# Two pairs of projection chunks by seven products instead of eight, the value section last

## What is computed

```python
z = _rmsnorm(x, norm_g) @ w_in                       # (512 + 8, 1024) @ (1024, 4096)
rq, rk, rv, rg, sq, sk, sv, sg = jnp.split(z, 8, axis=-1)
rq = _rope(rq.reshape(b, l, H_RET, HEAD_DIM), pos)   # rk likewise
o_ret, s_new = _retention(rq, rk, rv, s0)
sq = _rmsnorm(sq.reshape(b, l, H_SB, HEAD_DIM), sb_qn_g)   # sk likewise
o_sb = _sb_attention(sq, k_all, v_all, pos, k_pos)   # samples: paged key and value cache, 64 pages each
mix = jnp.concatenate([o_ret * jax.nn.silu(rg), o_sb * jax.nn.silu(sg)], axis=-1)
return x + mix @ w_out, s_new, sk, sv
```

## Time and profile before

| what | value |
|---|---|
| median of three runs | 962.53 us |
| the profiled execution, its own time | 960.3 us |
| its span, first to last instruction | 958.7 us |
| PE, DVE, ACT, POOL busy | 911.0, 480.1, 293.2, 249.2 us |
| the projection of layer 0, first matmul to last row | 10.1 to 253.2 us |
| mean granted TensorE clock | 0.985 |

### The profile page before, as it was taken

The page is one execution under the profiler, slowest core; times in us unless marked ns, Lnnn a source line. Parts: engine busy times, 40 slices in busy tenths (PEclk is TensorE's granted clock), DMA queues, the critical chain, the costliest instruction groups (busy, mean ns, idle before and its releaser), DMA issues.

```text
span 958.7 us, 15899 instructions
## 1 busy us (share of the span) xinstructions
PE 911.0 (95%) x5224; PEld 484.8 (51%) x5224; DVE 480.1 (50%) x965; ACT 293.2 (31%) x716; POOL 249.2 (26%) x353
## 2 busy tenths in 40 slices
PE   8999999999899999999999999998899998887998
PEld 4444444444455553545565676566554444444444
DVE  1248777779344643212133262724677775776211
ACT  6111111103454541032101110433565564655000
POOL 0000223200033430340424242000443354357000
PEclk9999999999999999999999999999899997999999
DMA  9333666593154457782414142030122232033211
GB/s 356 105 126 119 226 226 192 189 287 79 45 147 158 138 193 271 255 195 91 135 42 146 34 143 87 13 90 12 42 60 66 65 94 97 1 92 108 92 45 45
DMA packets 82487, 117.61 MB, mean 123 GB/s; under 512 B 21006, under 2 KB 45790, under 8 KB 82094
## 3 DMA queue, kind: packets, MB, share of 16 engines
q1 hardware_dynamic: 61824, 78.87, 25.2%
q0 software_dynamic: 10944, 29.41, 10.4%
q10 hardware_dynamic: 9648, 8.41, 2.7%
HBM read 108.70 MB, written 11.36 MB: 125 GB/s over the span
## 4 chain that ended last, share of the span: by engine, by line
PE 84%; DVE 6%; DMA 3%; ACT 3%; issue 2%; POOL 1%; POOLq 1%; SPq 0%; ACTq 0%; DVEq 0%
PE ps L729 26%; PE ps L989 11%; PE ps L995 6%; PE ps L1293 6%; PE ps L1012 4%; PE ps L738 4%; PE ps L1051 3%; PE ps L927 3%; PE ps L1163 3%; PE ps L1174 3%; DMA arena<-cache_sb_v 2%; PE ps L905 2%; DVE work L2000 2%; PE ps L877 2%; PE ps L1029 1%
## 5 line engine op out<-in xcount | busy, mean ns | idle before, releaser
L729 PE MATMUL ps<-wring,arena 128*128 128x512 f32 x448 | 195.3, 594 | 1.5 <-issue 1.5
L729 PEld LDWEIGHTS ps<-wring,arena 128*128 128x128 f32 x448 | 84.1, 190 | 104.0 <-issue 103.9
L668 POOL TENSOR_TENSOR z<-z,work 128x1024 f32<-128x1024 f32 (+1 forms) x64 | 80.1, 1254 | 159.6 <-DVE work L2008 159.3
L989 PE MATMUL ps<-wring,z 128*128 128x512 f32 (+2 forms) x320 | 106.7, 488 | 0.0
L1525 ACT ACTIVATE z<-ps,work 128x512 f32<-128x512 f32 (+3 forms) x128 | 66.4, 525 | 72.0 <-DVE work L2000 69.8
L1348 ACT ACTIVATE z<-ps 128x512 f32<-128x512 f32 (+1 forms) x64 | 27.4, 433 | 181.8 <-PE ps L729 147.5
L360 POOL DMA_DIRECT2D arena<-cache_sb_k x64 | 34.4, 537 | 164.1 <-DVE work L1643 141.6
L989 PEld LDWEIGHTS ps<-wring,z 128*128 128x128 f32 x320 | 54.8, 190 | 43.4 <-issue 41.8
L1848 DVE TENSOR_TENSOR arena<-ps,consts 128x512 f32<-128x512 f32 x32 | 30.3, 1020 | 82.3 <-PE ps L1029 82.3
L1805 DVE TENSOR_TENSOR xres<-xres,ps 128x512 f32<-128x512 f32 (+1 forms) x32 | 15.5, 484 | 86.4 <-PE ps L1293 38.9
L1012 PE MATMUL ps<-arena,wring 64*128 64x512 f32 (+3 forms) x256 | 54.3, 502 | 4.2 <-ACT z L1525 4.2
(11 more groups left out here) (322 smaller groups left out, 1272.5 us busy)
## 6 DMA issues: line engine op xcount, KB each, us to landing
wring<-w_in SPq DMA_DIRECT2D x12, 2048.0 KB, 11.1
arena<-cache_sb_k POOLq DMA_DIRECT2D x64, 256.0 KB, 3.1
arena<-cache_sb_v SPq DMA_DIRECT2D x64, 256.0 KB, 3.7
wring<-w_out SPq DMA_DIRECT2D x3, 2048.0 KB, 7.9
arena<-cache_sel_k SPq DMA_DIRECT2D x64, 64.0 KB, 1.8
consts<-aux SPq DMA_DIRECT2D x1, 2315.5 KB, 15.1
xres<-x_prompt SPq DMA_DIRECT2D x4, 512.0 KB, 8.0
wring<-w_in SPq DMA_DIRECT2D x2, 1024.0 KB, 7.1
```

What stands on the lines that cost most here:

```text
L668: nc.gpsimd.tensor_tensor(P_u(n), P_u(n), bc(coef(n).unsqueeze(2), [P, 2, (NT - n % NT) * P]), ALU.mult).then_inc(n_scaled, 1)
L729: mm = pe.matmul(ps[:, t, 0:width], stat, mov, start=(k == 0), stop=(k == KT - 1))
L989: mm = pe.matmul(ps[:, bank, at:at + w], normed1(k, t), wring[:, slot, k, lo:lo + w], start=(k == 0), stop=(k == KT - 1))
```

## The change

The sections are renumbered: SQ, SK, SG, RQ, RK, RV, RG and SV last. The pairs (SQ, SK) and (RQ, RK) are computed by Strassen's scheme in Winograd's form: x is cut into two token halves and two k halves (A11, A12, A21, A22), the two sections' weights into quarters of 1 MB (b11, b21, b12, b22), and seven products of 256 tokens x 512 k x 512 columns stand for eight. A product is two token tiles of four matmuls. VectorE makes four sums of x once (S1 to S4), four sums of weights per pair (T1, T2, T3, T4) and ten sums of 512 columns of products per pair. The other sections are computed as before. Other edits:

- The key pages are issued by SP, and two pages share one product and one reduction on VectorE; the page loop is cut into five parts with the second pair's sums between them.
- SP's order: after the second pair's weights (mm_done waits) the first key pages, half of RV's weights, all other key pages, the retention state, the first value pages, the samples' retention values; then o4 and o6; o5 and o7 after SV is evicted; then o3 and the other value pages.
- ACT's queue issues the other quarters of RV, RG and SV. SG's and half of RV's weights lie in parts of z that are not yet written.
- SV is computed last, in banks 5 and 4 by turns, with `sb_turn(0, 0)` before it, `front(0)` after its tile 0, `front(1)` after tile 1, `rs_turn` and `ds_sums` after tile 2. The copies of q and k go to ACT; `softplus(0)` goes to DVE's place after `rotate(RK)`; the sample's softplus chain stands between the two rotations. In the loop's first step `rs_sums` stands behind the retention's first turn.

```diff
-SQ, SK, SV, SG, RQ, RK, RV, RG = range(8)
+SQ, SK, SG, RQ, RK, RV, RG, SV = range(8)
...
 # SP
+                sp.wait_ge(mm_done, MM_PAIR[0] + 14)
+                for q, section, half in ((3, RK, 1), (2, RK, 0)):
+                    quarter_load(q, section, half)
+                sp.wait_ge(mm_done, MM_PAIR[0] + 16)
+                for half in range(2):
+                    quarter_load(half, RQ, half)
+                load_pages(sp, "cache_sb_k", page_loaded, 0, 0, 1)
+                sp.wait_ge(mm_done, MM_PLAIN[SG] + 5)
...
+                load_pages(sp, "cache_sb_k", page_loaded, 0, 1, NB * NPG // 4)
                 sp.wait_ge(ds_scores, 1)
...
+                sp.wait_ge(sections_ready, 2)
+                store(outs["o4"]..., z[:, 0:NT, SK * HW:(SK + 1) * HW])
+                store(outs["o6"]..., sec(NT, SK))
+                sp.wait_ge(bank_free, 5 + 5 * NCHUNK0)
+                store(outs["o5"]..., z[:, 0:NT, SV * HW:(SV + 1) * HW])
+                store(outs["o7"]..., sec(NT, SV))
                 sp.wait_ge(rs_S, 1)
...
 # PE
+                def product(bank, x, w, t, onto=False):
+                    for k in range(KT // 2):
+                        mm = pe.matmul(ps[:, bank, :], xpart(x, k, t), w[:, k], start=(k == 0 and not onto), stop=(k == KT // 2 - 1),
+                                       skip_group_check=True)
+                    mm.then_inc(mm_done, 1)
+                def pair(p):
+                    free, loads = FREE_PAIR[p], 16 * (p + 1)
+                    made, before = DVE_PAIR[p], DVE_PAIR[0]
+                    pe.wait_ge(q_loaded[0], loads)
+                    for t in range(2):
+                        if p == 0:
+                            turn_x(0, t)
+                            pe.wait_ge(xnT_ready, t + 1)
+                        else:
+                            pe.wait_ge(bank_free, FREE_PLAIN[SG] + t + 1)
+                        product(t, "A11", quarter(0), t)
+                    pe.wait_ge(q_loaded[1], loads)
+                    for t in range(2):
+                        if p == 0:
+                            turn_x(0, 2 + t)
+                        pe.wait_ge(bank_free, free + 1 + t)
+                        product(t, "A12", quarter(1), t, onto=True)
+                    if p == 0:
+                        turn_x(0, NT)
+                        pe.wait_ge(xnT_ready, NT + 1)
...
+                    plain_rows(4, from_quarters(0, 1))
...
+                    plain_rows(5, from_quarters(2, 3))
+                    pe.wait_ge(dve_sum, 1 if p == 0 else before + 8)
+                    for t in range(2):
+                        product(2 + t, "S4", quarter(3), t)
+                    pe.wait_ge(dve_sum, made + 1)
+                    for t in range(2):
+                        pe.wait_ge(dve_sum, before + 9 + t) if p else None
+                        product(6 + t, "S3", t3_sum, t)
+                    pe.wait_ge(dve_sum, made + 2)
+                    for t in range(2):
+                        pe.wait_ge(bank_free, free + 7 + t)
+                        product(2 + t, "S1", quarter(2), t, onto=True)
+                    pe.wait_ge(dve_sum, made + 3)
+                    for t in range(2):
+                        pe.wait_ge(bank_free, free + (6, 5)[t])
+                        product((5, 4)[t], "S2", quarter(0), t)
+                    pe.wait_ge(dve_sum, made + 4)
+                    for t in range(2):
+                        pe.wait_ge(bank_free, free + 9 + t)
+                        product(6 + t, "A22", quarter(1), t, onto=True)
...
+                pair(0)
+                plain(SG, from_sections, freed_by_pair(0), turned_out=True)
+                pair(1)
+                plain(RV, from_section_and(3), freed_by_pair(1))
+                plain(RG, from_quarters(2, 0), lambda t: (bank_free, FREE_PLAIN[RV] + t + 1))
+                sb_turn(0, 0)
                 for t in range(NT):
+                    pe.wait_ge(bank_free, FREE_PLAIN[SV] + (0, 0, 1, 2)[t])
+                    plain_tile(SV, t, 5 - t % 2, w_sv)
+                    if t == 0:
+                        front(0)
                     if t == 1:
+                        front(1)
+                    if t == 2:
                         rs_turn()
                         ds_sums()
+                plain_rows(5, w_sv)
                 pe.wait_ge(zeroed, 1)
                 pe.wait_ge(ds_a, 1)
...
 # DVE
+                st.done(TT(xsum["S1"], half[2], half[3], ALU.add))
+                st.done(TT(xsum["S2"], xsum["S1"], half[0], ALU.subtract))
+                turned_x(0, NT)
+                st.done(TT(xsum["S4"], half[1], xsum["S2"], ALU.subtract))
+                TT(xsum["S3"], half[0], half[2], ALU.subtract).then_inc(dve_sum, 1)
+                weight_sums(0, 0, 4)
...
+                pair_sums(0, 0)
+                pair_sums(0, 1)
                 head_norm(SQ, "gain_sq")
+                def page_products(first, last):
+                    with st.loop(last - first, 2, first=first) as r:
+                        for v in range(2):
+                            for u in (2 * v, 2 * v + 1):
+                                dve.wait_ge(page_loaded[u], r * 16 + 16)
+                            TT(work[:, 0:2 * CH]..., pages[:, 2 * v:2 * v + 2, :], bc(qbc..., [P, 2, CH]), ALU.mult).then_inc(page_free, 2)
+                            dve.wait_ge(page_free, r * 4 + (4 + 2 * v + 2))
+                            st.done(RED(zs[:, ...], heads(work[:, 0:2 * CH]), AX.X, ALU.add))
                 head_norm(SK, "gain_sk")
+                weight_sums(1, 0, 1)
+                page_products(0, 3)
+                weight_sums(1, 1, 4)
+                page_products(3, 7)
+                pair_sums(1, 0)
+                page_products(7, 8)
+                pair_sums(1, 1)
+                page_products(8, NB * NPG // 4)
                 TS(zs, zs, SCALE, None, ALU.mult).then_inc(ds_scores, 1)
                 rotate(RQ, 3)
...
+                rotate(RK, 4)
+                softplus(0)
```

```diff
+                leave(sec(0, SV), ps[:, 5, :], m + 1)
                 tail_of(0)
+                leave(sec(1, SV), ps[:, 4, :], m + 2)
+                leave(sec(2, SV), ps[:, 5, :], m + 3)
+                act.wait_ge(ds_la, 1)
+                tail_of(1)
+                leave(sec(3, SV), ps[:, 4, :], m + 4)
+                leave_rows(SV, 5, m + 5)
                 act.wait_ge(ds_lasum, 1)
                 nc.scalar.activation(zs, zs, ACT.Exp).then_inc(ds_a, 1)
-                tail_of(1)
```

More of the change, by code:

```diff
@@ L748, in project, with plain_tile @@
                     project_rows(n, slot, turned, before, width)
-                def second_half():
-                    pe.wait_ge(w_loaded[0], 16)
-                    turn_x(0, 1)
+                def plain_tile(section, t, bank, weights, turned_out=False):
+                    for k in range(KT):
+                        if turned_out:
+                            stat, mov = weights(k)[:, t * P:(t + 1) * P], xnT[:, k, 0:SEQ]
+                        else:
+                            stat, mov = by_token(k, t), weights(k)
+                        mm = pe.matmul(ps[:, bank, :], stat, mov, start=(k == 0), stop=(k == KT - 1))
+                    mm.then_inc(mm_done, 1)
@@ new lines, in plain_rows @@
+                def plain_rows(bank, weights):
+                    for k in range(KT):
+                        for row, a, e in quarters(0, CH):
+                            mm = pe.matmul(ps[row:row + NB, bank, 0:e - a], xnT[:, k, SEQ:SEQ + NB], weights(k)[:, a:e],
+                                           start=(k == 0), stop=(k == KT - 1))
+                    mm.then_inc(mm_done, 1)
+                def product(bank, x, w, t, onto=False):
+                    for k in range(KT // 2):
+                        mm = pe.matmul(ps[:, bank, :], xpart(x, k, t), w[:, k], start=(k == 0 and not onto), stop=(k == KT // 2 - 1),
+                                       skip_group_check=True)
+                    mm.then_inc(mm_done, 1)
@@ new lines, in leave, with leave_rows @@
+                def leave(dst, src, event, func=ACT.Copy):
+                    act.wait_ge(mm_done, event)
+                    nc.scalar.activation(dst, src, func).then_inc(bank_free, 1)
+                def leave_rows(section, bank, event):
+                    act.wait_ge(mm_done, event)
+                    for row, a, e in quarters(0, CH):
+                        ins_ = nc.scalar.activation(sec(NT, section)[:, a:e], ps[row:row + NB, bank, 0:e - a],
+                                                    ACT.Silu if section in (SG, RG) else ACT.Copy)
+                    ins_.then_inc(bank_free, 1)
@@ new lines, in pair @@
+                def pair(p):
+                    (sA, sB), m = PAIRS[p], MM_PAIR[p]
+                    if p:
+                        for t in range(2):
+                            leave(sec(2 + t, sB), ps[:, t, :], m + 1 + t)
+                    for t in range(2):
```

(19 more changed lines are left out.)

301 lines of the change are left out of this document (189 added, 112 removed).

## The result

The changed kernel takes **968.41 us** (median; 963.63 to 973.8) against 961.83 for the kernel before on the same chip: a ratio of 1.0068 [1.0048, 1.0089]. 968 was predicted, in a range of 957 to 977; the sign (slower) holds too, though by little over the half per cent that can be told. The profiled execution took 967.65 (span 966.0), so against the one of before its span grew by 7.3.

A forecast was written before the change was run, and what follows sets the result against it. TensorE was taken to bound the kernel, busy 95% of the span. Delays of 2.5 us up to the attention loop's start, 1.9 for value pages and 1.0 for clock sum to 5.4 on the 962.53 median: 968 us, range 957 to 977.

The forecast's parts named there:

- PE's saving: TensorE in layer 0's projection: seven products instead of eight save 6.92 us per pair, 13.8 us in all.
- DVE's lateness: VectorE before the transposes of q and k: both rotations ready at 240.2, 9 us after TensorE asks; 245.2 with page waits.
- Page waits s: VectorE's page loop in layer 0: time waiting for key pages beside ScalarE's weight loads, taken as 5 us.
- scaled 7: Page loop: waits of 7 us for 5 MB of weights, scaled at 1.4 per MB from an earlier 11.3 us.
- rival 4: SP cannot feed the page loop: page waits of 8 to 13 us, 971 to 979 us; chance 0.18.
- estimate of 2.5: Page loop: with equal shares between queues a page pair lands in about 4 us, so waits near 2.5 us.
- T to L: From TensorE resuming at the transposes (T, 245.2) to the attention loop's start (L, 260.5): 15.3 us, L 2.5 later.
- Behind L: After the attention loop's start: second-group value pages 1.9 us later behind stores on SP, plus 1.0 us for TensorE's clock.
- The 4.4 us issue: SP's queue after the attention loop's start: upper case, a store issue of 4.4 us makes the delay 5.
- 3: Page waits of 3 to 8 us in layer 0's page loop, giving 965 to 971 us; chance 0.42.
- 1: Saving arrives: VectorE not late at the transposes, rotations ready by 231, loop start 244, 948 to 952 us; up to 957: 0.13.
- 2: VectorE late at the transposes, but no page waits and little clock loss: 959 to 961 us; chance 0.27.

The follow-up runs named there:

- the control: Kernel before with key rotation on GpSimd, value stores behind the last value page and the sample's retention values sent and read back first: 961.77 us, ratio 1.0022.
- Light loads: Changed kernel with ScalarE's five quarter loads bringing 64 of each 512 columns, 0.6 MB instead of 5 MB: 963.35 us, ratio 1.0002.
- the runs above: Changed kernel with value stores behind the last value page, 960.21 us; changed kernel with eleven filler products ahead of the turns, 969.59 us.
- the retention values first: Changed kernel with key rotation on GpSimd, value stores behind the value pages, retention values sent and read back before state and pages: 948.96 us, ratio 0.9865.

## Why the prediction was right, step by step

- **PE's saving** held. PE reached the turns of q and k at 232.24; 231.1 was predicted. PE's busy time in the projection fell by 10.0 us (from 243.7 to 233.7, counted from 8 us to the last row), not by about 14: the low clock behind the idle adds 2.1 to it. Where DVE is in time, the whole change is worth 12.8 to 15.1, by the control.
- **DVE's lateness** was right in kind and 2.4 us too large: ready at 242.8, not 245.2. The sum without page waits was some 3.5 too high: the scaling ended at 216.59, less 6.4 of waits 210.2, where 213.7 stood. Loop entries were counted at 0.4 each, 2.0 in all; the first page product follows pair 1's first weight difference without a gap (100.63 + 2.29 = 102.9). The loop's turn of 0.65 was counted for 16 iterations, but in five parts it stands only 12 times, 2.6 less; against this DVE's last sum of pair 0 ended 0.9 later than the 69.7 predicted. The iteration was right (167.31 to 173.27, 5.96; predicted 5.92), and so were rotations with the softplus chain (26.2; predicted 26.45).
- **Page waits s**: 6.4, where 5 was taken, from the rows of the heavy loads. Light loads take 4.5 of it away, so the term's cause was right too; but 1.9 stay, where the prediction had 0 without contention (its 2.6 us is of one page alone, not two). The scaled 7 was read too high: the 11.3 of the earlier trace rows hold the loop's own turn four times, 8.6 are left, and five quarters come to 5.4. And 6.4 is one execution: with the same page loop the runs above had 8.1 and 8.8, past the 8 at which rival 4 begins. The estimate of 2.5 from equal turns of the queues, by the Trainium skill's "DMA: Bandwidth & Descriptors", section on queues, rings and completion order, was far too low here: beside the quarter loads pages took 5.3 and 5.7 us on the chain (at 136.33 and 143.85). Rival 4's cause falls: with SP still issuing, light loads leave 1.9, and issuing from the other queue makes it worse.
- **T to L**: 15.2, predicted 15.3. The clock's part was taken as 2.3; from the turns to the next tile it is 4.52 us (242.84 to 247.36) in the changed kernel, 2.41 without idle (231.55 to 233.96): 2.1. The rule of the Trainium skill's "TensorE: Matmul & The Clock Gate", section on HAM oscillation, that weighed against the change there, agrees with the trace. L came at 258.05, 2.4 ahead of the 260.5, all of it DVE's.
- **Behind L** is the step that was mis-sized: 1.9 for the pages and 1.0 for the clock, together 2.9, against 4.6. The place was right (the stores ahead of the second group on SP's queue), but the state's store was priced at its 2.32 for two issues, and behind the value stores its second issue alone took 4.29; table reads and checks took 4.2 (263.38 to 267.56), not 2.9. The 4.4 us issue stood in the prediction as the upper bound; that is the case that came, with another store. The second clock drop came as well (0.50 in 268 to 272).
- **Layer 1**'s 1.7 was in no term. The same drop at that place is in six of ten profiled executions of the changed kernel and its variants, and in neither of the kernel before and its variant; the idle that precedes it is the same 1.41 us. Why it comes stays open.
- The sum, 5.4 against a span grown by 7.3 and medians 6.6 apart, is right in part by luck, because errors offset each other: 2.4 too late at L against 1.7 too little behind it and 2.6 further on that no term had.
- **Rivals**: 3, the forecast, holds 968.4 in its 965 to 971. 1 is the version with DVE unburdened (L 246.14 without the prompt's rotations, 244 predicted), but not this kernel; behind L its plus 2 became minus 2.2 once the stores were moved. 2 did not come: s was above the 3 from which the forecast decides.

## What to carry to other kernels

Work taken from the bounding engine pays only if the engine that feeds its next step has as much slack as the saving: here 13.8 us of TensorE met a VectorE that had 2 us in hand, and moving 12 us of VectorE's work and two stores turned, with one small transfer, a loss of 0.7% into a gain of 1.3%. Look also at what a reordered section takes with it: a store that is ready only at the end stands in front of loads on its queue, and its issue is paid by whoever waits for those loads. And run the repairs on the old kernel too: only that tells a gain of the change from one of the repairs.

## What the runs showed of the hardware

- A store issue on SP can block the queue for longer than a page takes to land: behind the 1 MB value store the second half of the state's store took 4.29 us, and both halves 5.00 (4.98 in the run with the key rotation on GpSimd alone); with the value stores moved behind, both took 2.4.
- GpSimd beside VectorE: 1.23 us became up to 2.19 for products with both operands in SBUF, while reductions with one operand kept 1.22. The Trainium skill's "SBUF — State Buffer", section "Who interferes with whom", says the same of these two kinds of instruction; the trace agrees. Key rotation on GpSimd so cost the page loop 3.3 us (39.2 us of products became 42.5) while it freed DVE of 11.8.
- Kernels with the same opening begin up to 4 us earlier or later, most of it by what the clock grants to the first products (3.70 us for eight records at a granted clock of 1.00 in the changed kernel, 6.37 at 0.50 with the retention values first). Two profiled executions are to be compared from a common instruction on, not from the span's start.
